# Token-routed experts whose fill and end are reordered, with the last router products reversed, and a chunked recurrence solved on four quadrants of the array

## The chip, the cores and the metric

One core of one Trainium2 chip runs the whole program in one launch. The metric is the device time of one execution in microseconds (us): the median of three runs. TensorE is called PE, VectorE DVE, ScalarE ACT, GpSimd POOL, and SyncE, which issues most transfers, SP.

## The reference

The reference is two model blocks in a row on a sequence of 1024 tokens of width 1024. Of the first block, two places matter here. `x @ w_out` gives a residual; its norm goes through a router (36 columns: 4 groups and 32 experts), and every token goes to 2 of 32 experts of hidden width 512:

```python
y = (silu(x @ w_gate[e]) * (x @ w_up[e])) @ w_down[e]      # for each token, its 2 experts
```

Of the second block, what matters is an RWKV recurrence over 8 heads of 64 x 64 in two directions:

```python
def rwkv_step(S, inp):
    r, w, k, v, kk, a = inp
    sa = einsum('dbhvk,dbhk->dbhv', S, -kk)
    S = S * w[..., None, :] + sa[..., :, None] * (kk * a)[..., None, :] + v[..., :, None] * k[..., None, :]
    return S, einsum('dbhvk,dbhk->dbhv', S, r)
```

The kernel computes the recurrence in 16 chunks of 64 steps. Within a chunk the dependence of the steps on each other is a strictly triangular matrix N, and what is needed is its inverse (I - N)^-1, a product of (I + N^(2^i)) over six levels.

## The kernel before, in words

Stages follow each other; each one has its own buffers and a block in which the five engines run their own instruction lists and wait for each other by semaphores. Between two stages all engines meet.

**The stage "go"** (`deep_norm`, from L3906) is the product with `w_out`. Row tiles of 128 tokens go through it in pairs. For each row tile it also computes the norm, transposes it (`turn`, L4035), splits it into a high and a low part on ACT (L4125) and DVE (L4207), and takes the router's logits: 24 products, each with 128 x 128 values of the norm as the loaded weights and 36 router columns streamed. For the last pair all of this comes after the pair's products, with nothing beside it; DVE then copies the logits (L4243) and the stage is over.

**The stage "moe"** (`moe`, from L1436) runs one step per tile of 128 token rows, 33 steps here, in a loop; step j does the gate and up products of tile j and the down product of tile j-1. Step 0 is written out, the later ones are a loop with a test at each step (`steps`, L1479), on every engine. A product takes three PE passes (high x low, low x high, high x high, `products3`, L157 to L159), so all weights are split: ACT writes the high part (`high`, L1629) and DVE the low part (`half`, L1775), in two halves (q) of 128 x 2048 values for each of the three weights. The rest of a step on ACT: `Silu` of the gate product (L1644), the high parts of the turned activation (L1647) and of the turned token rows (L1650), half of the output y (L1655), and the issue of the store of y (L1662), which waits for both halves of y. On DVE: the low part of the activation (L1790), the product with the up half (L1794), the low part of the rows (L1796), the other half of y (L1801). SP issues the loads: the row tile (L1529), then the weights (L1520), each as its split buffer comes free. Before the tiles can be read, POOL scatters all token rows to their slots with 16 indirect transfers (L1813), which all count on one semaphore, `moved`. The rows being scattered lie where the high and low parts of the down weights are written later, so ACT waits for `moved` before its first split of down weights at the end of step 0, and DVE's follows from it; SP waits for `moved` at the end of step 0 too, before any load of step 1.

The order at the end of a step on ACT is: its half of y, the high part of the down weights (two instructions), the wait for both halves of y, the store. On DVE it is: the low part of the up weights, its half of y, the low part of the down weights.

**The stage "rs"** (`rw_scan`, from L2714) is the recurrence. Of each chunk there are 16 matrices (4 head pairs, 2 members, 2 directions). For a chunk PE does: `prepare` (L2815 to L2832), `score` (L2845), `output` (L2903), `solve` (L2913), level 0 of the next chunk's inverse (L2876, L2882), `update` (L2922, L2927), `values` (L2855), levels 1 to 5 (L2878 to L2882), and `ask` of the next chunk (L2890). A level has two groups (g); in each, a product Q of 64 x 64 values by a 128-column operand (the next power and the next partial inverse at once), and a product P of 64 columns (the power's transpose). Both members b of a matrix pair have input rows and output rows in the same half of the partitions, so the level products use two of the array's four 64 x 64 quadrants. ACT copies Q (L2973) and group 1's P (L2974), DVE group 0's P (L3020), and DVE adds the partial inverse (L3026). A level starts when the copies of the one before have landed. `prepare`, `ask` (L2890) and the products of L2832 take their input rows from one half and write to either, four quadrants in turn. Every product here is f32 and shows as two MATMUL records.

```python
                    for e in range(RP):
                        for b in range(2):
                            d, p, o, k = e // 2, e % 2 * 2 + b, home[b], g * RP + e
                            ...
                                pe.matmul(p_q[g][o, e], pm[o, k], qx[o, k], start=True, stop=True)
```

Of the kernel before, what the change touches and what calls it, by code (L numbers as in the profile page):

```python
# [21 lines left out]
ALU = mybir.AluOpType  # L22
# [1413 lines left out]
def moe(nc, logits, consts, tri_strict, ones, h2, h2_rows, xs, ys, gate2, slots, tile_exp, ident, w_gate, w_up, w_down):  # L1436
# [5 lines left out]
    with Stage(nc, "moe") as s:  # L1442
# [29 lines left out]
        moved = s.sem("moved", soft=True)  # L1472
# [33 lines left out]
        def _(sp):  # L1506
# [15 lines left out]

            def ahead(j, b, k, n_used):
# [3 lines left out]
                if not first:  # L1527
                    sp.wait_ge(turned, past(j))
                    sp.dma_start(x[:, 1 - b], xs.rearrange("(j p) n -> j p n", p=P)[j + 1],  # L1529
                                 cond=(n_used > j + 1)).then_inc(x_in[1 - b], 16)  # L1530
# [26 lines left out]
            steps(sp, 1, step)  # L1557
# [63 lines left out]
        def _(act):  # L1621
# [50 lines left out]
        def _(v):  # L1672
# [113 lines left out]
            def step(j, b, k, n_used):  # L1786
                first = isinstance(j, int) and j == 0
                if not first:
                    v.wait_ge(at_hi, past(j))
# [12 lines left out]
                low(d_hi, d_lo, wd, wd_hi, wd_lo, j + 1)  # L1802
# [3 lines left out]
        def _(pool):  # L1806
# [4 lines left out]
            for t in range(NT):  # L1811
                for k in range(2):
                    pool.indirect_dma_start(xs[:, :], bass.IndirectOffsetOnAxis(ap=slots[:, k, t:t + 1], axis=0),  # L1813
                                            h2_rows[:, t], None).then_inc(moved, 16)
# [899 lines left out]
def rw_scan(nc, vecs, vs3, first, first_in, vT, el, sc_mask, p_mask, ident, yT):  # L2714
# [11 lines left out]
    with Stage(nc, "rs") as s:  # L2726
# [4 lines left out]
        sc, pm, qx = s.sb("sc", [P, 2, ND, 2, P]), s.sb("pm", [P, ND, RC]), s.sb("qx", [P, ND, P])  # L2731
# [4 lines left out]
        (turned, v_turned, p0_done, scored, level, z_done, u_done, s_done, y_done, bk_ok, v_ok, u_ok, lv_q,  # L2736
         lv_p0, lv_p1, p0_ok, sc_ok, x1_ok, lv_dve, zs_ok, s_ok, y_ok) = (s.sem(n) for n in (
             "turned", "v_turned", "p0_done", "scored", "level", "z_done", "u_done", "s_done", "y_done", "bk_ok",
             "v_ok", "u_ok", "lv_q", "lv_p0", "lv_p1", "p0_ok", "sc_ok", "x1_ok", "lv_dve", "zs_ok", "s_ok", "y_ok"))
# [6 lines left out]
        p_q, p_p = [wide(n) for n in range(2)], [banks[:, 2 + n] for n in range(2)]  # L2746
# [26 lines left out]
        def q_level(n, lv, g):  # L2773
            return (n * (NL - 2) + lv) * 2 + g + 1

        def p_level(n, lv):
            return n * (NL - 1) + lv + 1

        def dve_level(n, lv, g):
            return (n * (NL - 1) + lv - 1) * 2 + g + 1  # L2780
# [21 lines left out]
        def _(pe):  # L2802
            def prepare(n):
# [6 lines left out]
                if n:  # L2810
                    for g in range(2):
                        pe.wait_ge(lv_dve, past(dve_level(n - 1, NL - 1, g)))
# [6 lines left out]
                if n:  # L2819
                    pe.wait_ge(lv_p0, past(p_level(n - 1, NL - 2)))  # L2820
# [5 lines left out]
                if n:  # L2826
                    pe.wait_ge(lv_p1, past(p_level(n - 1, NL - 2)))
# [31 lines left out]
            def raise_power(n, lv):  # L2859
                for g in range(2):  # L2860
                    if lv == 0:
                        pe.wait_ge(sc_ok, past(2 * n + 2))
                    else:
                        if lv < NL - 1:
                            pe.wait_ge(lv_q, past(q_level(n, lv - 1, g)))
# [1640 lines left out]
```

## Time and profile before

| | us |
|---|---|
| median of three runs (4133.52 to 4139.69) | 4139.14 |
| the profiled execution, its own time | 4142.12 |
| its span | 4140.3 |
| PE busy in the span | 3631.0 (88%) |
| DVE busy | 2830.5 (68%) |
| ACT busy | 1609.6 (39%) |
| mean granted clock of PE | 0.936 |

A row of the timeline gives the start and the duration in us, the engine, the line, the operation, the tiles written and read, and in brackets how long the engine was idle before it and what released it. A row with x2 or more merges neighbours: its duration runs from the first start to the last end. MATMUL durations hold some 0.22 us of pipeline, so products that start 0.03 us apart overlap. PEld is the load of weights. PEclk is the clock that PE was granted, as a share of 2.4 GHz.

### The profile page before, as it was taken

Reading aid. Unit: us, or ns where it says so; the run is one execution under the profiler, and the core shown is the slowest. Engines: PE = TensorE matmul, PEld = TensorE weight load, DVE = VectorE, ACT = ScalarE, POOL = GpSimd, SP = SyncE. Lnnn points to the kernel's source line nnn. Section 1 sums busy time; section 2 is a strip of 40 time slices with the busy share of each in tenths; the row PEclk is TensorE's granted clock in tenths of the full one; section 3 lists DMA queues with packets and bytes.
Section 4 is the critical chain, followed back from the end, with each engine's and each line's share of the span. In section 5 each row is a group of like instructions: output and inputs, shape, how many; then the busy total and the mean of one; then the engine's idle time right before and its main releaser. Section 6 shows DMA issues by size and latency. Waiting matters only on the chain. (4 is left out here: it accounts for less than half of the span.)

```text
span 4140.3 us, 62371 instructions
## 1 busy us (share of the span) xinstructions
PE 3631.0 (88%) x24735; PEld 2927.8 (71%) x24735; DVE 2830.5 (68%) x3464; ACT 1609.6 (39%) x2136; POOL 72.4 (2%) x56
## 2 busy tenths in 40 slices
PE   6999996879959999948999776649999897999897
PEld 4888885767848888836888432319997676888786
DVE  4775325977559999978886588685555557667356
ACT  3222212545537777754333120253333133322244
POOL 0000000000020000010000000000000000000000
PEclk8999998999969999978999888779999998999999
DMA  5942225536579999953332331340111332222565
GB/s 199 337 166 92 88 76 194 192 112 214 181 278 420 413 411 411 399 194 102 102 122 102 124 123 69 117 166 26 42 34 63 102 117 77 82 91 73 187 192 170
DMA packets 262498, 689.49 MB, mean 167 GB/s; under 512 B 30136, under 2 KB 126072, under 8 KB 235754
## 3 DMA queue, kind: packets, MB, share of 16 engines
q1 hardware_dynamic: 226474, 559.75, 37.8%
q10 hardware_dynamic: 20528, 67.11, 4.3%
q0 software_dynamic: 15248, 59.14, 3.9%
q8 instruction: 177, 2.90, 0.3%
q14 instruction: 71, 0.58, 0.0%
HBM read 530.81 MB, written 172.96 MB: 170 GB/s over the span
## 5 line engine op out<-in xcount | busy, mean ns | idle before, releaser
L157 PE MATMUL g_ps<-h1T_hi,g_w_lo 128*128 128x512 f32 x448 | 175.4, 392 | 6.9 <-DVE g_w_lo L356 6.9
L1775 DVE TENSOR_TENSOR moe_wg_lo<-moe_wg,moe_wg_hi 128x2048 fp32r<-128x2048 f32 x68 | 153.1, 2288 | 35.6 <-ACT moe_wg_hi L1629 35.5
L159 PE MATMUL g_ps<-h1T_hi,g_w_hi 128*128 128x512 f32 x448 | 174.8, 390 | 0.0
L158 PE MATMUL g_ps<-h1T_lo,g_w_hi 128*128 128x512 f32 x448 | 174.8, 390 | 0.0
L4164 DVE TENSOR_TENSOR x3T_lo<-fd_w_raw,x3T_hi 128x1024 fp32r<-128x1024 f32 x66 | 80.8, 1224 | 122.6 <-ACT x3T_hi L4093 122.4
L1775 DVE TENSOR_TENSOR moe_wu_lo<-moe_wu,moe_wu_hi 128x2048 fp32r<-128x2048 f32 x68 | 152.9, 2288 | 16.3 <-ACT moe_wu_hi L1629 16.3
L1775 DVE TENSOR_TENSOR moe_wd_lo<-moe_wd,moe_wd_hi 128x2048 fp32r<-128x2048 f32 x66 | 148.3, 2289 | 14.9 <-ACT moe_wd_hi L1629 14.9
L2882 PE MATMUL rs_banks<-rs_pm,rs_qx 64*64 64x64 f32 x2048 | 157.2, 217 | 0.0
L157 PE MATMUL fd_acc<-x3T_hi,x3T_lo 128*128 128x512 f32 x352 | 139.2, 395 | 19.9 <-DVE x3T_lo L4167 19.9
L157 PE MATMUL g_ps<-x2T_hi,g_w_lo 128*128 128x512 f32 x352 | 139.8, 397 | 17.1 <-DVE g_w_lo L583 17.1
L157 PE MATMUL g_ps<-g_w_hi,h1T_lo 128*128 128x512 f32 x384 | 149.6, 390 | 0.0
L158 PE MATMUL g_ps<-g_w_lo,h1T_hi 128*128 128x512 f32 x384 | 149.4, 389 | 0.0
L159 PE MATMUL g_ps<-g_w_hi,h1T_hi 128*128 128x512 f32 x384 | 149.4, 389 | 0.0
L2882 PEld LDWEIGHTS rs_banks<-rs_pm,rs_qx 64*64 64x64 f32 x2048 | 143.6, 133 | 0.0
L158 PE MATMUL g_ps<-x2T_lo,g_w_hi 128*128 128x512 f32 x352 | 139.8, 397 | 0.0
L159 PE MATMUL g_ps<-x2T_hi,g_w_hi 128*128 128x512 f32 x352 | 139.2, 396 | 0.0
L158 PE MATMUL fd_acc<-x3T_lo,x3T_hi 128*128 128x512 f32 x352 | 138.7, 394 | 0.0
L159 PE MATMUL fd_acc<-x3T_hi 128*128 128x512 f32 x352 | 138.7, 394 | 0.0
L402 DVE COPY g_st<-g_ps 128x512 f32<-128x512 f32 x24 | 16.6, 691 | 176.4 <-PE g_ps L159 176.4
L1629 ACT ACTIVATE moe_wg_hi<-moe_wg 128x2048 fp32r<-128x2048 f32 x68 | 127.0, 1920 | 16.6 <-DMA moe_wg<-in_exp_w_gate 16.6
L4093 ACT ACTIVATE x3T_hi<-fd_w_raw 128x1024 fp32r<-128x1024 f32 x66 | 70.0, 1060 | 160.6 <-PE fd_acc L159 112.8
L2878 PE MATMUL rs_banks<-rs_qx,rs_pm 64*64 64x128 f32 x1536 | 131.2, 272 | 0.0
(738 smaller groups left out, 10776.4 us busy)
## 6 DMA issues: line engine op xcount, KB each, us to landing
moe_wg<-in_exp_w_gate SPq DMA_DIRECT2D x68, 1024.0 KB
moe_wu<-in_exp_w_up SPq DMA_DIRECT2D x68, 1024.0 KB
moe_wd<-in_exp_w_down SPq DMA_DIRECT2D x66, 1024.0 KB
fd_w_raw<-in_ffn_w_down SPq DMA_DIRECT2D x66, 512.0 KB, 4.5
go_w_raw<-in_w_out SPq DMA_DIRECT2D x64, 512.0 KB, 4.4
g_w<-in_w_in SPq DMA_DIRECT2D x52, 512.0 KB, 4.8
g_w<-in_w_in SPq DMA_DIRECT2D x22, 1024.0 KB, 7.7
s_xs<-g_zero POOLq DMA_DIRECT2D x2, 8192.0 KB, 34.3
```

The lines of the kernel that those rows point to most:

```text
L157: pe.matmul(out, l[1], r[0], start=(k == 0), stop=False)
L158: pe.matmul(out, l[0], r[1], start=False, stop=False)
L159: return pe.matmul(out, l[0], r[0], start=False, stop=(k == kt - 1))
L402: v.tensor_copy(st[:, j % 2, 2 * i + 1], ps[:, 2 * i + 1]).then_inc(by_dve, 1)
L1629: act.activation(hi[:, q * m:q * m + m], w[:, q * m:q * m + m], ACT.Copy).then_inc(sem_hi, 1)
L1775: v.tensor_tensor(lo[:, q * m:q * m + m], w[:, q * m:q * m + m], hi[:, q * m:q * m + m], ALU.subtract).then_inc(sem_lo, 1)
L2878: pe.matmul(p_q[g][o, e], pm[o, k], qx[o, k], start=True, stop=True)
L2882: mm = pe.matmul(p_p[g][o, e], q, pm[o, k], start=True, stop=True)
L4093: act.activation(w_hi[:, n % NB], w_raw[:, n % NR], ACT.Copy).then_inc(w_high, 1)
L4164: v.tensor_tensor(w_lo[:, n % NB], w_raw[:, n % NR], w_hi[:, n % NB], ALU.subtract).then_inc(w_low, 1)
```

## The change

In "moe": `moved` becomes two semaphores, one for the first eight scatter transfers and one for the last eight. ACT's and DVE's splits of the down weights go from the end of step j to the start of step j+1, behind a wait for `moved[0]` on ACT and `moved[1]` on DVE. At the end of a step ACT waits that the down weights have landed and for y, and issues the store. SP's step 1 is written out; in it the load of row tile 2 stands behind four weight loads and behind the wait for both `moved`. In "go": the products of the last pair load the router's 36 columns as weights and stream 128 rows; ACT copies the result and PE transposes it into the logits. In "rs": for one of two head groups (`par` 1) the halves of the partitions alternate with the level, so that the products of a level go to four quadrants; all products have 64 columns, in three kinds (P, its transpose Q, and the partial inverse X = X(I + N^(2^i)), for which DVE makes `rx` = power + I); the copies are one of 128 x 384 for each group and parity, three on ACT and one on DVE. The groups g are now the directions.

```diff
@@ moe @@
-        moved = s.sem("moved", soft=True)
+        moved = [s.sem(f"moved{n}", soft=True) for n in range(2)]
@@ sync: ahead() and step() @@
-                if not first:
+                if not isinstance(j, int):
                     sp.wait_ge(turned, past(j))
-                    sp.dma_start(x[:, 1 - b], ...).then_inc(x_in[1 - b], 16)
+                    rows_x(j, b, n_used)
...
+                if isinstance(j, int) and j == 1:
+                    sp.wait_ge(turned, past(j))
+                    for m in moved:
+                        sp.wait_ge(m, 16 * NT)
+                    rows_x(j, b, n_used)
                 for q in range(2):
                     if not first:
                         sp.wait_ge(d_lo, past(j * 2 + (q - 1)))
...
-                if isinstance(j, int) and j == 0:
-                    sp.wait_ge(moved, 16 * 2 * NT)
...
-            steps(sp, 1, step)
+            steps(sp, 2, step)
@@ scalar: step() @@
+                if not first:
+                    act.wait_ge(moved[0], 16 * NT)
+                    high(d_in, d_hi, wd, wd_hi, j * 16)
                 act.wait_ge(gated, past(j + 1))
...
                     act.activation(y[:, 1 - b, 0:512], p_y[:, 0:512], ACT.Copy).then_inc(y_act, 1)
+                for q in range(2):
+                    act.wait_ge(d_in[q], past(j * 16 + 16))
                 if first:
-                    act.wait_ge(moved, 16 * 2 * NT)
-                high(d_in, d_hi, wd, wd_hi, j * 16 + 16)
+                    act.nop()
                 if not first:
                     act.wait_ge(y_act, past(j + 1))
                     act.wait_ge(y_dve, past(j + 1))
@@ vector: step() @@
                 if not first:
+                    v.wait_ge(moved[1], 16 * NT)
+                    low(d_hi, d_lo, wd, wd_hi, wd_lo, j)
                     v.wait_ge(at_hi, past(j))
...
                     v.tensor_copy(y[:, 1 - b, 512:], p_y[:, 512:]).then_inc(y_dve, 1)
-                low(d_hi, d_lo, wd, wd_hi, wd_lo, j + 1)
@@ rw_scan @@
-        p_q, p_p = [wide(n) for n in range(2)], [banks[:, 2 + n] for n in range(2)]
+        def powers_of(g, par):
+            return banks[:, 2 * g + par]...[:, 0:6 * RC]...
+        def place(b, par, lv):
+            return other[b] if par and lv % 2 else home[b]
@@ tensor: raise_power() @@
+                    else:
+                        pe.wait_ge(lv_act, past(act_at(n, lv - 1, 3 if g else 1)))
+                        if g == 0:
+                            pe.wait_ge(lv_dve, past(dve_at(n, lv - 1)))
+                    members = [(par * RP + g * 2 + a, a, b, par) for a in range(2) for par in range(2) for b in range(2)]
...
+                    if lv < NL - 1:
+                        for k, a, b, par in members:
+                            mm = pe.matmul(to(a, b, par, 0), power(k, a, b, par), pm[place(b, par, lv), k], start=True, stop=True)
+                    if lv < NL - 2:
+                        for k, a, b, par in members:
+                            mm = pe.matmul(to(a, b, par, 1), pm[place(b, par, lv), k], power(k, a, b, par), start=True, stop=True)
+                    if lv:
...
+                        pe.wait_ge(lv_r, past(r_at(n, lv - 1, g)))
+                        for k, a, b, par in members:
+                            o = place(b, par, lv)
+                            mm = pe.matmul(to(a, b, par, 2), rx[o, k], xm[o, k], start=True, stop=True)
@@ scalar: raise_power() @@
+                for g, par in ((0, 0), (1, 0), (1, 1)):
                     act.wait_ge(level, past(at_level(n, lv, g)))
+                    act.activation(own(px[:, :, c], g, par), powers_of(g, par)[:, :, c], ACT.Copy).then_inc(lv_act, 1)
@@ vector: raise_power() @@
+                v.tensor_copy(own(px[:, :, c], 0, 1), powers_of(0, 1)[:, :, c]).then_inc(lv_dve, 1)
+                if lv < NL - 1:
+                    v.drain()
+                    for g in range(2):
+                        v.wait_ge(lv_act, past(act_at(n, lv, 3 if g else 1)))
+                        ...
+                        v.tensor_tensor(both[0], both[1], bc(eye...), ALU.add).then_inc(lv_r, 1)
@@ deep_norm: tensor, last pair @@
-                for t in passes[-1]:
-                    rate(t)
+                for i, t in enumerate(passes[-1]):
+                    pe.wait_ge(by_dve, past(t + 1))
+                    for k in range(ND):
+                        mm = products3(pe, acc[0:nf, t % n_acc, 0:P], [h[:, k] for h in (f_hi, f_lo)],
+                                       [h[:, t % 2, k] for h in (t_hi, t_lo)], k, ND)
+                    mm.then_inc(pair_done, 1)
+                for i, t in enumerate(passes[-1]):
+                    pe.wait_ge(pair_ok, past(i + 1))
+                    mm = pe.transpose(pl[:, t, 0:nf], pair[0:nf, t % 2], ident[0:nf, 0:nf])
+                mm.then_inc(rated, 1)
```

## Rows read from the trace of the kernel before

**Rows 1.** Windows: us, then busy us (count) of PE, PEld, DVE, ACT, POOL; PEclk, DMA, GB/s
```profile
1145.00:1158.00 13.00, 12.00 (x56) 11.92 (x56) 1.72 (x3) 1.02 (x1) 0.00 (x0) 0.50 0.01 1
...
1245.00:1797.00 552.00, 552.00 (x2591) 458.84 (x2589) 505.19 (x309) 415.53 (x307) 0.00 (x0) 1.00 0.95 389
...
2790.00:3175.00 385.00, 373.39 (x10242) 357.86 (x10239) 217.06 (x449) 125.37 (x304) 0.00 (x0) 0.99 0.10 31
```

**Rows 2.** Timeline of one step of the experts on ACT and DVE
```profile
1780.03 3.71 ACT L1629 ACTIVATE moe_wd_hi<-moe_wd 128x2048 fp32r<-128x2048 f32 x2
1781.12 0.68 DVE L1801 COPY moe_y<-moe_p_y 128x512 f32<-128x512 f32 x1
1781.97 4.49 DVE L1775 TENSOR_TENSOR moe_wd_lo<-moe_wd,moe_wd_hi 128x2048 fp32r<-128x2048 f32 x2 [0.17 <-ACT moe_wd_hi L1629]
1782.02 0.34 ACTq L1662 DMA_DIRECT2D s_ys<-moe_y  x1
...
1787.90 4.50 DVE L1775 TENSOR_TENSOR moe_wg_lo<-moe_wg,moe_wg_hi 128x2048 fp32r<-128x2048 f32 x2 [0.83 <-ACT moe_wg_hi L1629]
...
1794.62 4.49 DVE L1775 TENSOR_TENSOR moe_wu_lo<-moe_wu,moe_wu_hi 128x2048 fp32r<-128x2048 f32 x2 [0.49 <-ACT moe_wu_hi L1629]
```

**Rows 3.** Line L1801, DVE's half of y: all instructions, ns min/median/max, first and last start
```profile
L1801 DVE COPY moe_y<-moe_p_y x32: 680/684/685, 1243.3 to 1799.0; 128x512 f32<-128x512 f32 x32
```

**Rows 4.** Timeline at the experts' fill, ACT
```profile
1220.51 3.71 ACT L1629 ACTIVATE moe_wd_hi<-moe_wd 128x2048 fp32r<-128x2048 f32 x2 [9.99 <-DMA s_xs<-h_rows,slots]
```

**Rows 5.** Timeline at the experts' end: the next stage's first instruction
```profile
1809.17 0.35 SPq L1874 DMA_DIRECT2D nf_r<-s_x  x1
```

**Rows 6.** Timeline of the last router products
```profile
1146.71 0.38 PE L157 MATMUL go_pl<-go_f_hi,go_t_lo 128*128 128x36 f32 x1
...
1148.16 1.22 DVE L4207 TENSOR_TENSOR go_t_lo<-go_pt,go_t_hi 128x1024 fp32r<-128x1024 f32 x1 [3.18 <-ACT go_t_hi L4125]
...
1157.16 0.46 DVE L4243 COPY logits<-go_pl 128x288 f32<-128x288 f32 x1 [7.78 <-PE go_pl L159]
```

**Rows 7.** Timeline of one chunk of the recurrence: where its levels lie
```profile
2937.79 0.33 PE L2876 MATMUL rs_banks<-rs_sc,rs_pm 64*64 64x64 f32 x4
...
2938.00 1.21 ACT L2980 ACTIVATE rs_uv<-rs_p_z 64x512 f32<-64x512 f32 x2 [3.50 <-PE rs_p_z L2913]
...
2939.80 1.15 PE L2922 MATMUL rs_p_s<-rs_uv,rs_bk 128*64 128x64 f32 x32
...
2942.57 0.33 PE L2878 MATMUL rs_banks<-rs_qx,rs_pm 64*64 64x128 f32 x2
...
2943.96 0.43 PE L2878 MATMUL rs_banks<-rs_qx,rs_pm 64*64 64x128 f32 x4
...
2944.21 0.38 ACT L2973 ACTIVATE rs_qx<-rs_banks 128x256 f32<-128x256 f32 x1 [3.65 <-PE rs_banks L2882]
...
2951.40 0.42 DVE L3026 TENSOR_TENSOR rs_qx<-rs_qx,rs_banks 128x256 f32<-128x256 f32 x1 [0.92 <-ACT rs_qx L2973]
...
2951.97 0.34 PE L2880 MATMUL rs_banks<-rs_qx,rs_pm 64*64 64x64 f32 x4 [0.16 <-DVE rs_qx L3026]
...
2955.02 0.37 PE L2815 MATMUL rs_banks<-k_ident,rs_cm 64*128 64x64 f32 x5
```

**Rows 8.** Timeline: 64 x 64 products on four quadrants (L2832) and on two (L2903, L2913)
```profile
2956.97 0.34 PE L2832 MATMUL rs_banks<-rs_cm 64*64 64x64 f32 x9
...
2959.84 0.50 PE L2903 MATMUL rs_banks<-rs_cm,rs_st 64*64 64x64 f32 x10
...
2960.36 1.10 PE L2913 MATMUL rs_p_z<-rs_zs,rs_qx 64*64 64x64 f32 x32
```

**Rows 9.** Lines of ACT and DVE in one chunk: busy us, mean ns | idle before
```profile
L2973 ACT ACTIVATE rs_qx<-rs_banks 128x256 f32<-128x256 f32 x8 | 3.1, 382 | 8.3 <-PE rs_banks L2882 8.3
...
L2959 ACT ACTIVATE rs_bk<-rs_banks 128x512 f32<-128x512 f32 x2 | 1.1, 595 | 2.2 <-PE rs_banks L2815 2.2
...
L3020 DVE COPY rs_pm<-rs_banks 128x256 f32<-128x256 f32 x5 | 2.1, 422 | 1.9 <-PE rs_banks L2882 1.9
```

More of the change, by code:

```diff
@@ L2730, in rw_scan @@
         bk, uv = s.sb("bk", [P, 2, ND, P]), s.sb("uv", [P, 2, ND, 2, RC])
-        sc, pm, qx = s.sb("sc", [P, 2, ND, 2, P]), s.sb("pm", [P, ND, RC]), s.sb("qx", [P, ND, P])
+        sc, px = s.sb("sc", [P, 2, ND, 2, P]), s.sb("px", [P, ND, 3 * RC])
+        pm, qm, xm = (px[:, :, c * RC:c * RC + RC] for c in range(3))
+        rx, eye = s.sb("rx", [P, ND, RC]), s.sb("eye", [P, RC])
         zs, st = s.sb("zs", [P, ND, RC]), s.sb("st", [P, ND, RC])
@@ L2771, in at_level, with act_at, dve_at, r_at @@
             return (n * NL + lv) * 2 + g + 1
[L2773 to L2780, printed above, removed]
+        def act_at(n, lv, i):
+            return (n * NL + lv) * 3 + i
+        def dve_at(n, lv):
+            return n * NL + lv + 1
+        def r_at(n, lv, g):
+            return (n * (NL - 1) + lv) * 2 + g + 1
+        def columns(lv):
+            return slice(0, 2 * RC) if lv == 0 else slice(0, 3 * RC) if lv < NL - 1 else slice(2 * RC, 3 * RC)
+        def own(ap, g, par):
+            return ap[:, par * RP + 2 * g:par * RP + 2 * g + 2]
         home = [half[1], half[0]]
         other = [half[0], half[1]]
+        def place(b, par, lv):
+            return other[b] if par and lv % 2 else home[b]
         units = [(2 * a + b, a, b, q ^ b) for a in range(RP // 2) for q in range(2) for b in range(2)]
@@ L2810, in prepare @@
                 if n:
-                    for g in range(2):
-                        pe.wait_ge(lv_dve, past(dve_level(n - 1, NL - 1, g)))
+                    pe.wait_ge(lv_act, past(act_at(n - 1, NL - 1, 3)))
+                    pe.wait_ge(lv_dve, past(dve_at(n - 1, NL - 1)))
                 for d in range(2):
@@ L2907, in solve @@
                 pe.wait_ge(zs_ok, past(j + 1))
-                for g in range(2):
-                    pe.wait_ge(lv_dve, past(dve_level(j, NL - 1, g)))
+                pe.wait_ge(lv_act, past(act_at(j, NL - 1, 3)))
+                pe.wait_ge(lv_dve, past(dve_at(j, NL - 1)))
                 for d in range(2):
@@ L2968, in raise_power @@
             def raise_power(n, lv):
-                for g in range(2):
-                    k = slice(g * RP, g * RP + RP)
+                c = columns(lv)
+                for g, par in ((0, 0), (1, 0), (1, 1)):
                     act.wait_ge(level, past(at_level(n, lv, g)))
-                    if lv < NL - 2:
-                        act.activation(qx[:, k, 0:RC], p_q[g][:, :, 0:RC], ACT.Copy).then_inc(lv_q, 1)
-                act.activation(pm[:, k], p_p[1][:, 0:RP], ACT.Copy).then_inc(lv_p1, 1)
+                    act.activation(own(px[:, :, c], g, par), powers_of(g, par)[:, :, c], ACT.Copy).then_inc(lv_act, 1)
             def solved(j):
@@ L2982, in _ @@
             prepare(0)
-            for lv in range(NL - 1):
+            for lv in range(NL):
                 raise_power(0, lv)
@@ L2989, in _ @@
                 if j + 1 < NRC:
-                    for lv in range(NL - 1):
+                    for lv in range(NL):
                         raise_power(j + 1, lv)
@@ L2995, in _ @@
             v.memset(st[:, :, :], 0.0).then_inc(s_ok, 1)
+            for o in half:
+                v.tensor_copy(eye[o], ident[o, o])
+            v.drain()
             v.wait_ge(m_in, past(32))
@@ L2999, in prepare @@
                 v.wait_ge(p0_done, past(n + 1))
-                v.tensor_tensor(by_parity(pm[:, :, :]), banks[:, 3:5, 0:RP], by_parity(mp[:, :, :]), ALU.mult).then_inc(p0_ok, 1)
+                v.tensor_tensor(by_parity(pm), banks[:, 3:5, 0:RP], by_parity(mp[:, :, :]), ALU.mult).then_inc(p0_ok, 1)
                 if n >= 2:
@@ L4156, in _ @@
                     high(t)
+                for i, t in enumerate(g):
+                    act.wait_ge(pair_done, past(i + 1))
+                    act.activation(pair[0:nf, t % 2], acc[0:nf, t % n_acc, 0:P], ACT.Copy).then_inc(pair_ok, 1)
         @block.vector
```

73 lines of the change are left out of this document (30 added, 43 removed).

## The prediction

> **What bounds the kernel now.** I read the windows by stage first, because the change touches three stages with different limits. In the experts' steady part [rows 1] PE is busy for 552.00 of 552.00 us at the full clock, with DVE at 505.19 (92%) and DMA at 0.95. So PE bounds it, but DVE has only 8% to spare. In the recurrence [rows 1] PE is busy for 373.39 of 385.00 us, and DVE and ACT are far below. In the window of the last router products PE is busy too, but at 0.50 of the clock. Next the timelines. In one step of the experts [rows 2] the reader is to see how tightly ACT's high part of the down weights (1780.03) sits before DVE's low part (1781.97): DVE idles 0.17 us there, 0.83 before the gate weights and 0.49 before the up weights, 1.49 us a step in all. DVE's half of y repeats 32 times from 1243.3 to 1799.0 [rows 3]: 31 periods of 17.92 us.
>
> **The change, part by part.**
>
> *Experts, every step.* Before, ACT starts the high part of the down weights right after its own half of y and only then waits for DVE's half. After, the wait for DVE's half and the store stand ahead of it. DVE's half ends at 1781.12 + 0.68 = 1781.80; the store's issue ends at 1782.02 + 0.34 = 1782.36 [rows 2], so 0.56 us. Then the loop's test. No row shows a boundary with work behind it: from the DVE's last split (1799.0 + 0.68 + 4.49 = 1804.2, [rows 2, 3]) to the next stage at 1809.17 [rows 5] lie 15 empty passes, 0.33 us each at least; above, ACT's trace leaves room for 1.0. I take 0.6, as registers are computed too. Then the first high half, 1.91 (1780.03 to just before 1781.97, [rows 2]), and 0.03 of signal. DVE, which has nothing else to do at that point, idles 3.1 us in place of 0.17. Its other two gaps vanish, since ACT gets ahead of a later DVE: ACT would finish the gate half some 7.7 us after DVE's y, DVE asks for it at 8.2. DVE's own work from the start of the down split (1781.97) to the end of y (1799.0 + 0.68 = 1799.7) is 17.74 - 0.83 - 0.49 = 16.42. The period becomes 16.42 + 3.1 = 19.5 us, longer than PE's 17.92: DVE is the bound and PE waits for the split rows. That is 1.6 us a step and +50 us over 31 periods (ends: +40 with 0.3 for the test, +62 with 1.0). The added wait for the landed down weights costs nothing: their buffer is free once DVE's split has read it, 5 to 8 us into the period, and the wait stands at its end. Were they late, the store, the next high half and DVE behind it would be.
>
> *Experts, the fill.* ACT's 9.99 us of idle for the scatter [rows 4] goes, but DVE still waits for the last scatter at the start of step 1, with the low parts of the down and gate weights, the rows and y queued behind it, and SP's load of row tile 2 waits too. From that landing (1220.5) the DVE chain is the 16.42 from above, so y of step 1 would end at 1236.9 against 1243.3 + 0.68 = 1244.0: -7. Against it: SP now issues four weight loads of 1 MB (tile 2's) before the scatter has landed; at 389 GB/s [rows 1] they are worth 10.8 us of the same DMA engines, which could put the landing back by as much, +4. On POOL nothing is moved. I take -1, nearer to the late end, since the scatter's last transfers are issued while these loads run.
>
> *Experts, the end.* DVE's and ACT's splits of weights for a tile that doesn't exist go. DVE ends 4.49 us earlier, but ACT has 15 passes of its own after the store: 0 to -4.5, taken as -2.
>
> *Last router products.* 48 products run from 1146.71 to shortly before 1157.16 [rows 6], 0.213 us each at half clock, the pace of their 128-column weights. Reversed, 128 columns stream: a 512-column product takes 552/2591 = 0.213 at the full clock [rows 1], so 0.107 for 128 at half. The second tile can't start before its low part, 1148.16 + 1.22 = 1149.38 [rows 6]; 24 x 0.107 brings 1151.9, and the copy, a transpose and the pipeline some 1.6: 1153.5, -3.6. If the small weights load as slowly as the large, it is +1. I take -3; what follows on DVE is serial, so it reaches the end.
>
> *Recurrence, the rate.* Records on four quadrants start (0.34 - 0.22)/8 = 0.015 us apart (L2832), on two 0.031 (L2903) and 0.028 (L2913) [rows 8]; two records a product: 0.031 against 0.058. The products of a mid level are 48 of 64 columns now, where they were 16 of 128 and 16 of 64: 1.5 us of PE, where a level takes 2 x 1.35 = 2.7 us now (a group is 2943.96 back to about 2942.6, [rows 7]).
> A rule speaks against this. After the change two row halves write the same bank at the same time. L2903 does this already, at 0.031 against 0.028 for L2913, which alternates banks [rows 8]: it costs a tenth, not the gain. The Trainium skill (TensorEngine Tiling (Array Packing), Gotcha 1: PSUM Pressure) says that different row tiles cannot access the same PSUM bank simultaneously; by that the levels would stay at 0.058, a rival below.
>
> *Recurrence, the chain.* At this rate PE waits for copies. From the end of a group to ACT's start is 0.25 (2943.96 to 2944.21); from a DVE end (2951.82) to PE 0.15 [rows 7]. ACT copies 256 columns in 0.38, 512 in 0.60, so 384 in 0.49; DVE 0.42 and 0.68, so 0.56 [rows 3, 9]. Group 1 needs two ACT copies in a row, 0.88 with their overlap. Its cycle in levels 2 and 3: 0.25 + 0.88 + 0.15 + 24 x 0.031 = 2.0, plus 0.1 for DVE's sum with I, which X waits for: 2.1. In levels 4 and 5 that sum is bare: 0.25 + 0.88 + 0.03 + 0.42 + 0.15 + 0.25 = 2.0 each. Levels 1 to 5: 1.5 + 2.1 + 2.1 + 2.0 + 2.0 = 9.7, and `prepare` follows 0.9 later, after the last copies: 10.6 against 2955.02 - 2942.57 = 12.45 [rows 7]. -1.85 x 16 = -30. Level 0 runs from 2937.79 to 2939.80; `update` then needs ACT's copies, 2938.00 + 1.21 + 0.15 = 2939.36: -0.44 x 15 = -6. DVE's four small sums instead of two lie beside level 0. Sum -36. Ends: +18 if the products keep 0.058 (level slots 2.8, the chain behind levels 4 and 5), -90 if no copy were ever waited for.
>
> **The sum.** +50 - 1 - 2 - 3 - 36 = +8 us. The profiled execution took 4142.12, which gives 4150; it lies 3 us over the median of the runs, 4139.14, so the median comes to 4147.
>
> **The rivals.**
> *The experts' period stays PE's* (faster). It needs DVE's wait for the down split to stay under 1.49 us, its whole slack [rows 2]; against it stands the 1.91 of the high half alone. Sum -42: 4097. Chance 0.10.
> *The recurrence's chain is shorter than its copies read*: if a copy of 384 columns costs what one of 256 does and starts earlier, a level comes to 1.8, another -19, at the far end PE's own 1.5. It decides from 3.3 us saved a chunk. 4128, 4093 at the end of it. Chance 0.13.
> *Four quadrants don't pay* (slower): same-bank writes, or PE's clock granted at half in the new gaps, where it is 0.99 now. +18 for -36: 4201. Chance 0.10.
> *The forecast*: the loop stretches, the recurrence pays back most of it. 0.67, spread 4130 to 4168.
>
> **How the numbers follow.** A measurement of this kernel can tell 0.2% from no change, 8.3 us. The forecast lies on that edge: of its 0.67, 0.32 is slower, 0.31 the same, 0.04 faster. With the rivals: faster 0.04 + 0.10 + 0.10 = 0.24, same 0.31 + 0.03 = 0.34, slower 0.32 + 0.10 = 0.42. The range 4108 to 4170 leaves out the first rival and the last, 2 in 10.
>
> **What would show it.** In the experts: DVE's half of y every 19.5 us, the wait of DVE's down split for ACT's near 3 us a step, PE no longer busy throughout, the steady part near 600 us. In the recurrence: level records 0.015 to 0.02 apart, a chunk in 21.2 us where it took 23.5, ACT's copies as the releaser of level products. The logits' copy 3 us sooner after L4207. If y still comes every 17.9 us, the forecast is wrong and the kernel is faster by about 1%.

## The result and the profile after

The changed kernel takes 4187.14 us (median of 3, 4185.75 to 4189.05) against 4139.14 before: a ratio of 1.0114, interval 1.0098 to 1.0129. It is slower by 48 us, where 8 were forecast, and outside the range of 4108 to 4170. Its profiled span is 4185.4 us, 45.1 over that of before.

I read the windows by stage first. The columns are those of [rows 1].

```profile
1136.00:1148.00 12.00, 7.54 (x66) 6.79 (x66) 5.45 (x7) 2.65 (x5) 0.00 (x0) 0.72 0.27 107
1240.00:1832.00 592.00, 565.10 (x2577) 456.58 (x2575) 499.63 (x308) 414.02 (x310) 0.00 (x0) 1.00 0.94 359
2822.00:3222.00 400.00, 321.98 (x11760) 291.96 (x11760) 230.98 (x496) 164.66 (x384) 0.00 (x0) 0.92 0.10 30
```

The reader is to see two things. In the experts' steady part, 592 us where 552 were enough [rows 1], PE is no longer busy throughout. In the recurrence PE was busy for 373.39 of 385.00 us at a granted clock of 0.99; now it is busy for 321.98 of 400.00 at 0.92, for 15% more instructions, and the stage is longer. Since 1.00 and 0.50 are the clock's two levels, 0.92 means that about 16% of the stage, 64 us, ran at half.

The timeline of the experts, DVE in two steps:

```profile
1796.27 0.68 DVE L1814 COPY moe_y<-moe_p_y 128x512 f32<-128x512 f32 x1
1800.13 4.50 DVE L1786 TENSOR_TENSOR moe_wd_lo<-moe_wd,moe_wd_hi 128x2048 fp32r<-128x2048 f32 x2 [3.18 <-ACT moe_wd_hi L1636]
...
1815.68 0.68 DVE L1814 COPY moe_y<-moe_p_y 128x512 f32<-128x512 f32 x1
1819.30 4.50 DVE L1786 TENSOR_TENSOR moe_wd_lo<-moe_wd,moe_wd_hi 128x2048 fp32r<-128x2048 f32 x2 [2.94 <-ACT moe_wd_hi L1636]
```

And ACT in the same two:

```profile
1797.19 0.34 ACTq L1673 DMA_DIRECT2D s_ys<-moe_y  x1
1798.18 3.72 ACT L1636 ACTIVATE moe_wd_hi<-moe_wd 128x2048 fp32r<-128x2048 f32 x2 [5.74 <-issue]
...
1816.60 0.34 ACTq L1673 DMA_DIRECT2D s_ys<-moe_y  x1
1817.36 3.72 ACT L1636 ACTIVATE moe_wd_hi<-moe_wd 128x2048 fp32r<-128x2048 f32 x2 [5.50 <-DVE moe_y L1814]
```

DVE's copy of y ends at 1796.95, the store is issued at 1797.19, ACT's split of the down weights starts at 1798.18 and DVE's at 1800.13. DVE waits 3.18 or 2.94 us there, and nowhere else in the step: from 1800.13 to the end of the next copy, 1816.36, it works for 16.23 us. The line of the copy, its first and last start:

```profile
L1814 DVE COPY moe_y<-moe_p_y x32: 680/684/687, 1236.8 to 1834.9; 128x512 f32<-128x512 f32 x32
```

31 periods from 1236.8 to 1834.9 are 19.29 us each, against 17.92 [rows 3]. From the timeline, the logits' copy, the fill's first row on DVE and the next stage's first instruction, which answer to [rows 4 to 6]:

```profile
1147.71 0.46 DVE L4289 COPY logits<-go_pl 128x288 f32<-128x288 f32 x1 [2.32 <-PE go_pl L4117]
...
1221.22 4.49 DVE L1786 TENSOR_TENSOR moe_wd_lo<-moe_wd,moe_wd_hi 128x2048 fp32r<-128x2048 f32 x2 [18.35 <-DMA s_xs<-h_rows,slots]
...
1842.84 0.34 SPq L1886 DMA_DIRECT2D nf_r<-s_x  x1
```

The timeline of a stretch of levels in the recurrence, rows of PE and one of ACT's copies:

```profile
2979.72 0.46 PE L2903 MATMUL rs_banks<-rs_px 64*64 64x64 f32 x16
2980.00 0.29 PE L2906 MATMUL rs_banks<-rs_px 64*64 64x64 f32 x6
2983.15 0.39 PE L2906 MATMUL rs_banks<-rs_px 64*64 64x64 f32 x10 [2.86 <-issue]
2983.32 0.45 PE L2913 MATMUL rs_banks<-rs_px,rs_rx 64*64 64x64 f32 x16
2983.55 0.45 PE L2903 MATMUL rs_banks<-rs_px 64*64 64x64 f32 x16
...
2983.81 1.25 ACT L3003 ACTIVATE rs_px<-rs_banks 128x384 f32<-128x384 f32 x3 [3.54 <-PE rs_banks L2913]
...
2984.73 0.54 PE L2903 MATMUL rs_banks<-rs_px 64*64 64x64 f32 x16 [0.26 <-ACT rs_px L3003]
2985.03 0.67 PE L2906 MATMUL rs_banks<-rs_px 64*64 64x64 f32 x16
2985.46 0.67 PE L2913 MATMUL rs_banks<-rs_px,rs_rx 64*64 64x64 f32 x16
2985.88 0.43 PE L2903 MATMUL rs_banks<-rs_px 64*64 64x64 f32 x5
2987.16 0.58 PE L2903 MATMUL rs_banks<-rs_px 64*64 64x64 f32 x10 [0.85 <-issue]
```

Outside the pauses the rate is the forecast's: 16 records of L2903 and L2913 start (0.45 - 0.22)/15 = 0.015 us apart, 0.031 a product, and by the starts of the sets at 2983.32 and 2983.55 it is 0.029. But in the middle of a set of products whose operands are all there, PE stops for 2.86 us and waits for "issue", that is, for nothing that the profile shows. ACT waits 3.54 us behind it. Behind the pause the rate is the one of the half clock for a while: the set at 2983.32 is followed by the next 0.23 us later, the one at 2985.03 only 0.43 later. The window from there on, in the columns of [rows 1], has the granted clock at half:

```profile
2985.00:2995.20 10.20, 8.54 (x211) 7.50 (x204) 3.76 (x9) 4.10 (x11) 0.00 (x0) 0.50 0.02 4
```

The waits of the stage, us in total, times, longest:

```profile
ACT rs_px L3003 <- PE rs_banks L2913: 146.4, 123, 4.4
DVE rs_rx L3059 <- ACT rs_px L3003: 63.3, 64, 4.2
PEld rs_banks L2913 <- issue: 20.1, 21, 3.4
PEld rs_banks L2913 <- ACT rs_px L3003: 17.2, 22, 1.4
```

The copies wait for PE far more than PE waits for them. I then counted PE's instructions along the trace: weight loads, matmuls and the few of its sequencer. A pause here is the time from one instruction's start to the next one's. The pauses for nothing stand whole multiples of 256 instructions apart; four of them:

```
number of the instruction   start, us   pause, us
31802                        2983.15     3.08
32058                        2987.16     1.16
33338                        3009.14     1.41
33594                        3012.63     0.64
```

The DMA queues of the stage give the other half of it, queue and kind: packets, MB, share. First before, then after:

```profile
q8 instruction: 81, 1.33, 1.4%
```

```profile
q8 instruction: 93, 1.52, 1.6%
```

A packet is 1.52 MB / 93 = 16 KB, and 93 x 256 is 23808, where PE's records of the stage are 23776; before it is 81 x 256 = 20736 to 20718. So PE's program comes in blocks of 256 instructions over a DMA queue of its own, one packet each, and no two of them start less than 3.3 us apart in either trace. A product of 64 x 64 shows as two weight loads and two matmuls. Four quadrants want 256 instructions, 64 products, in 64 x 0.031 = 2.0 us. In the records of the stage PE stands still for over 0.5 us 78 times, 83.6 us in all; before 3 times, 4.0 us. Of the 78, 31 with 47.2 us are put down to "issue", and every one of them stands at the same place in the count of 256. Most of the others are waits for a copy.

### The profile page after: what moved, and what is told of

Same layout as the page of the kernel before. It is cut to its first block and busy times, and to the rows that moved or that the text cites. A ratio compares the mean times of both kernels' runs of the same rounds, so it can differ in the third digit from the quotient of the medians.

```text
span 4185.4 us, 65587 instructions
## 1 busy us (share of the span) xinstructions
PE 3578.4 (85%) x26273; PEld 2849.5 (68%) x26273; DVE 2835.4 (68%) x3512; ACT 1640.8 (39%) x2216; POOL 71.8 (2%) x56
## 5 line engine op out<-in xcount | busy, mean ns | idle before, releaser
L1786 DVE TENSOR_TENSOR moe_wd_lo<-moe_wd,moe_wd_hi 128x2048 fp32r<-128x2048 f32 x64 | 143.8, 2289 | 113.3 <-ACT moe_wd_hi L1636 94.9
L1636 ACT ACTIVATE moe_wd_hi<-moe_wd 128x2048 fp32r<-128x2048 f32 x64 | 119.1, 1908 | 179.8 <-issue 89.1
L3003 ACT ACTIVATE rs_px<-rs_banks 128x384 f32<-128x384 f32 (+2 forms) x288 | 111.4, 434 | 152.9 <-PE rs_banks L2913 146.4
L4210 DVE TENSOR_TENSOR x3T_lo<-fd_w_raw,x3T_hi 128x1024 fp32r<-128x1024 f32 x66 | 80.8, 1224 | 120.8 <-ACT x3T_hi L4136 120.6
L157 PE MATMUL fd_acc<-x3T_hi,x3T_lo 128*128 128x512 f32 x352 | 139.2, 395 | 18.1 <-DVE x3T_lo L4213 18.1
L1636 ACT ACTIVATE moe_wu_hi<-moe_wu 128x2048 fp32r<-128x2048 f32 x68 | 126.6, 1918 | 0.7 <-DMA moe_wu<-in_exp_w_up 0.7
```

The lines of the kernel that those rows point to most:

```text
L157: pe.matmul(out, l[1], r[0], start=(k == 0), stop=False)
L1636: act.activation(hi[:, q * m:q * m + m], w[:, q * m:q * m + m], ACT.Copy).then_inc(sem_hi, 1)
L1786: v.tensor_tensor(lo[:, q * m:q * m + m], w[:, q * m:q * m + m], hi[:, q * m:q * m + m], ALU.subtract).then_inc(sem_lo, 1)
L3003: act.activation(own(px[:, :, c], g, par), powers_of(g, par)[:, :, c], ACT.Copy).then_inc(lv_act, 1)
L4210: v.tensor_tensor(w_lo[:, n % NB], w_raw[:, n % NR], w_hi[:, n % NB], ALU.subtract).then_inc(w_low, 1)
```

## The experiments

The theories: the experts lose by the order of store and split; the recurrence's gain is lost to **supply**, blocks of instructions that come too slowly. The rivals: **contention** of four quadrants for the PSUM banks, a chain of waits that the new scan makes longer, or an effect of the three parts on each other.

**The parts alone.** Each is the kernel before with that part of the diff.

```diff
+ mm = products3(pe, acc[0:nf, t % n_acc, 0:P], ...)            # router alone: deep_norm's hunks
...
+ act.wait_ge(moved[0], 16 * NT); high(d_in, d_hi, wd, wd_hi, j * 16)    # experts alone: its hunks
...
+ return other[b] if par and lv % 2 else home[b]                # scan alone: rw_scan's hunks
```

> The kernel before with the reversed last router products alone. In the changed kernel the logits' copy came 9.5 us sooner, 4.0 of it already there at the first of these products and 5.5 gained in them. If the 5.5 are the reversal's (products at 0.107 us, then 0.060 once the clock is full), this run is 5 to 6 us faster than before, about 4134, and the whole stage after it moves with it. If instead the 4 us ahead of it belong to the change too, it is 9 us faster. Rival: the work of the experts' start waits for weights, not for the logits, and the run is within 2 us of before.

> The kernel before with the experts' reordering alone. My theory: the store's wait ahead of ACT's high part stretches the period of a step from 17.92 to 19.29 us, as in the changed kernel, 31 periods, +42 us; the fill costs +3 (the scatter lands 10 us later, the waits gone give 7 back), the end gives -2. Sum +43: 4182. Rival, DMA: the period is long because weights arrive late; then ACT's and DVE's waits for DMA would show tens of us in the steady part, and the sum could lie anywhere. Rival, cross effect of the other parts: this run alone would be well under +43.

> The kernel before with the recurrence on four quadrants alone. Instruction supply theory: PE's instructions come in blocks of 256, one per 3.3 us at best; the dense level products use one up in 2 to 2.6 us, so PE stands still at every 256th instruction. The stage then takes 17 us more, as in the changed kernel, with stalls of 1 to 3.5 us at multiples of 256 PE records: total +14 to +20, 4155. Chain theory (the copies' chain is longer than I read): the same loss, but spread over every level as waits for ACT or DVE, none at multiples of 256. Rival: in the changed kernel the loss came from the other two parts (shifted phases); then this run is at 36 us under before.

Measured, as medians beside before's 4139.33: router 4133.82 (ratio 0.9986, 0.9976 to 0.9995); experts 4182.31 (1.0108, 1.0091 to 1.0125); scan 4152.56 (1.0024, 1.0002 to 1.0046). The differences, -5.5, +43.0 and +13.2, add to +50.7, where the whole change has +48.0. The 2.7 between the sums is less than the intervals leave open, so no effect of the parts on each other shows. Two of the three lose, the scan by an interval that only just leaves out no change: one of its five runs was at 4134.97. Weights that come late are out as a cause of the experts' loss: in the steady steps of the experts alone DVE waits 31 times, 94.9 us in all, for ACT's down split, and no wait for a DMA is listed.

**Bursts.** Ahead of the recurrence's first chunk 512 products run whose operands have been there for long, on four quadrants, then 512 on two. Nothing waits for a copy.

```diff
+            for rep in range(32):
+                ... pe.matmul(banks[home[b], 3 + par, d * 2 + a], vec(...), vec(...))    # four quadrants
+            for rep in range(32):
+                ... pe.matmul(banks[half[par], 2, d * RP + p], vec(...), vec(...))       # two
```

> The kernel before with two bursts of PE work ahead of the recurrence, whose results are overwritten: 512 products of 64 x 64 by 64 on four quadrants, then 512 on two quadrants. Each product is 4 PE instructions (2 loads of weights, 2 passes), so each burst is 2048 instructions, 8 blocks of 256. Supply theory: the first burst begins at the short-run pace of 0.031 us a product, then falls to the pace of the blocks, 3.3 to 3.6 us per 64 products (0.052 to 0.056 each), with pauses at every 64th product, 26 to 29 us in all; the second, at 0.058 a product or 3.7 us per block, hardly pauses, 30 us. Rival, no supply limit: the first burst keeps 0.031 to 0.036 throughout, 16 to 18 us, and the second 30.

Measured: 4196.62 us in one run; the bursts took 28.0 and 30.6 us. In the first, with the idle before them:

```profile
2794.68 0.27 PE L2936 MATMUL rs_banks<-rw_first 64*64 64x64 f32 x2 [0.51 <-issue]
...
2798.16 0.27 PE L2936 MATMUL rs_banks<-rw_first 64*64 64x64 f32 x2 [1.38 <-issue]
...
2801.90 0.27 PE L2936 MATMUL rs_banks<-rw_first 64*64 64x64 f32 x2 [1.65 <-issue]
...
2805.65 0.27 PE L2936 MATMUL rs_banks<-rw_first 64*64 64x64 f32 x2 [1.65 <-issue]
```

```
instructions of the burst at which PE pauses:  429  685  941  1197  1453  1709  1965   (256 apart)
pause, us:                                    0.73 1.59 1.87  1.87  1.60  1.59  1.59
a product, us:  four quadrants 0.034 between the pauses, 0.055 with them
                two quadrants  0.059 between the pauses, 0.060 with them (0.6 us in all)
```

In the first burst the granted clock was 0.50 for the first 4.7 us; from the second pause on a product takes 0.029 us between the pauses ((3.74 - 1.87)/64). Contention gives no reason for pauses every 256 instructions; supply does. The rate that four quadrants hold is 0.055 us a product, 28.0 / 8 = 3.5 us a block of 64. That is hardly better than the 0.060 of two. (The expectations below call a pair of one weight load and one matmul a product; a product of mine is two such pairs, so their 27.3, 16.8 and 29.3 ns are my 0.055, 0.034 and 0.059 us.)

**A loop around the bursts.** Each burst as 4 passes over 128 products, two blocks.

```diff
-            for rep in range(32):
+            with pe.Fori(0, 4):
+                for rep in range(8):
```

> The kernel with the two bursts of 1024 products each ahead of the recurrence, but each burst a loop of 4 passes over 256 products (512 instructions, two blocks of 256). Written out, the burst on four quadrants took 28.0 us, 27.3 ns a product, with a pause of 1.6 to 1.9 us every 256 instructions and 16.8 ns a product between them. Theory: the pauses are the fetch of a block of instructions. In a loop of two blocks the first pass pays them and the later ones do not: 7 + 768 x 0.0168 = 20 us for the first burst (up to 24 with the loop's own jumps), with no fetches in it after the first pass; the second burst, on two quadrants, stays at 29 to 30 ns a product. Rival: the pauses are the array's or the queue's own, every 256 instructions whatever their source: 28 us as before.

Measured: the first burst took 18.4 us in place of 28.0. Its first pass still went at 0.054 us a product with one pause of 0.96, and with the granted clock at 0.50 for its first 4.3 us; the passes behind it at 0.029, with 0.15 us at each jump. The windows of both bursts, first written out, then looped:

```profile
2788.60:2816.80 28.20, 18.80 (x1027) 17.82 (x1029) 0.00 (x0) 0.00 (x0) 0.00 (x0) 0.91 0.15 52
2816.80:2847.30 30.50, 30.34 (x1031) 30.04 (x1023) 0.00 (x0) 0.00 (x0) 0.00 (x0) 1.00 0.02 5
```

```profile
2794.30:2812.90 18.60, 17.72 (x1025) 17.46 (x1025) 0.00 (x0) 0.00 (x0) 0.00 (x0) 0.88 0.22 75
2812.90:2843.00 30.10, 30.10 (x1034) 30.03 (x1028) 0.00 (x0) 0.00 (x0) 0.00 (x0) 1.00 0.00 1
```

The instruction queue over the two bursts, in the same order:

```profile
q8 instruction: 16, 0.26, 1.8%
```

```profile
q8 instruction: 4, 0.07, 0.5%
```

The same products, the same banks, a quarter of the packets, and past the first pass the pauses are gone. So they are not a stop every 256 instructions whatever their source. Two quadrants gain nothing from the loop. The total, 4197.42, does not show it: the looped kernel came to the burst 5.7 us later, left the recurrence 4.6 us earlier, and the rest went in later stages that the edit does not touch.

**The scan on two quadrants.** The new scan's instructions in the same order, every operand in its home half.

```diff
-            return other[b] if par and lv % 2 else home[b]
+            return home[b]
```

> Before with the new scan, but every level's operands stay in their home half: the same instructions in the same order, on two quadrants in place of four. Theory: instructions come to TensorE at no more than 256 in 3.4 us, 27 ns for a product of two instructions, and on two quadrants a product takes 29 ns: four quadrants gain next to nothing, so this kernel is at most 6 us slower than the one on four, 4150 to 4159 us. Rival: the four quadrants do gain what the burst shows between its pauses (16.8 against 29.3 ns a product), and the loss is elsewhere: 16 chunks of some 200 products by 12 ns, 38 us slower than on four, over 4180 us.

Measured: 4158.31 us (1.0048, 1.0034 to 1.0062), 5.7 behind the scan on four. As written, four quadrants are worth 5.7 us by the medians, which the spread of the runs hardly separates (4135 to 4156 against 4155 to 4161), and 10.4 by the stage in the profiled runs (393.5 against 403.9); the forecast had them worth 54 (-36 against +18). On two quadrants only 5 pauses over 0.5 us are left that go to "issue", 5.6 us in place of 41.6.

**The scan in a loop.** TensorE's levels 1 to 4 as two passes over two levels, so that two levels' instructions a chunk need no fetching. Level 4 then computes one product more than it needs, and the waits whose value depends on the pass stand on instructions of their own. The flat kernel is its control, the same but for the loop.

```diff
+            def raise_powers(n):
+                with pe.Fori(0, 2) as i:          # flat: for i in range(2)
+                    for lv in (1, 2):
+                        raise_power(n, lv, i)     # waits for values of level lv + 2 * i
+                raise_power(n, NL - 1)
...
-                    for lv in range(1, NL):
-                        raise_power(j + 1, lv)
+                    raise_powers(j + 1)
```

> Before with the new scan, TensorE's levels 1 to 4 written as a loop of two passes over two levels (level 4 then computes one product more than it needs); the four waits of a group stand on instructions of their own. It takes about 190 instructions a chunk out of what is fetched (of some 1490), 13.4 ns each, 2.6 us of a chunk. Theory: the pauses every 256 instructions are what took the scan's gain, so the stage gets shorter than the written-out scan's by 10 to 35 us of its 399: 4117 to 4145 us in all (written out 4152.6), and fewer pauses over 0.5 us in TensorE's records. Rival: the pauses lie beside waits for the copies and cost the chain nothing: 4152 or, with the loop's jumps and the added waiting instructions (16 chunks by about 0.5 us), up to 4162.

> The same kernel as the one with the loop, with its two passes written out: the same products, the same waiting instructions, nothing looped. Both theories: 4153 to 4165 us, the written-out scan's 4152.6 and some more instructions (32 of products and some 16 waits a chunk, at 13.4 ns, 16 chunks: 10 us). Its difference to the looped kernel is the loop's alone: by the fetch theory 15 to 40 us, by the rival none or below nothing.

Measured: looped 4137.63 us (0.9997, 0.9988 to 1.0007), flat 4183.34 (1.0103, 1.0084 to 1.0122). The loop alone is worth 45.7 us, more than I had expected, since the flat kernel lost 31 us to its added instructions and not 10. Against the scan as it was written it is 15 us. The instruction queue of the stage, looped and then flat:

```profile
q8 instruction: 74, 1.21, 1.3%
```

```profile
q8 instruction: 97, 1.59, 1.5%
```

The stage took 372.9 us looped and 428.3 flat; 393.5 for the scan as written, 382.2 before. The pauses over 0.5 us come to 57.6 us looped (there are real waits for copies among them), 94.3 flat, 80.8 as written. Those put down to "issue" alone are 22.9 us looped, 60.0 flat and 41.6 as written. This is the same kernel with 23 blocks fewer to fetch, so supply is shown to be what turned the scan's gain into a loss. It is not shown that the whole -36 would come without it: the looped stage is 9.3 us shorter than before's, and how the rest divides between the pauses that are left, the extra product, the half clock and the copies' chain stays open. The granted clock moves with the pauses: in 350 us from 2800 on, first looped, then flat:

```profile
2800.00:3150.00 350.00, 294.65 (x11681) 271.46 (x11685) 219.31 (x474) 156.24 (x364) 0.00 (x0) 0.98 0.09 30
```

```profile
2800.00:3150.00 350.00, 280.39 (x10335) 256.81 (x10325) 192.89 (x414) 137.82 (x322) 0.00 (x0) 0.90 0.10 31
```

Over the whole stage the clock was granted at half for 18.1 us looped, 100.5 flat, 55.4 as written, 4.8 before, and 3.9 on two quadrants, where the pauses are few as well. How much of the 45.7 is the pauses themselves and how much the half clock behind them, no run separates; if work at half clock takes twice as long, the 82 us less of it are worth at most 41 (an estimate).

**The loop on two quadrants.** The looped scan with `place` as in the scan on two.

> The looped scan on two quadrants: every operand stays in its home half, everything else as in the looped kernel. Written out, two quadrants stood 5.7 us behind four (4158.3 to 4152.6), 10.4 in the profiled stages (403.9 to 393.5). Theory: four quadrants gain more once fewer instructions have to be fetched, since on two the array (29 ns a product) and not the fetch sets the pace, so there the loop brings little: 4153 to 4165 us, 15 to 27 behind the looped kernel's 4137.6. Rival: the loop helps both alike (it is a gain of its own, not one that frees the quadrants): 4143 us, 6 behind.

Measured: 4177.41 us (1.0091, 1.0074 to 1.0108), 40 behind the loop on four. That is over my 15 to 27, because I had not priced level 4's extra product: L2894, as that line was numbered there, is 1536 matmuls and 62.0 us busy in the scan on two quadrants, and L2898 here 2048 and 85.8, so up to 24 us, as PE is busy for 329.44 of 350 us here; on four quadrants the same is 53.0 to 62.4. So the 40 hold by estimate some 14 us that are the product's and not the fetch's. The rest, 25, still stands against 5.7 in the written-out pair: four quadrants pay once the instructions are there. No written-out kernel with the extra product ran on two quadrants, so the split of the 40 is an estimate.

**The order of store and split.** Before, with the wait for y and the store ahead of ACT's split; the split stays at the end of the step.

```diff
-                high(d_in, d_hi, wd, wd_hi, j * 16 + 16)
                 if not first: ... (waits for both halves of y, store)
+                high(d_in, d_hi, wd, wd_hi, j * 16 + 16)
```

> Before, with one change: at the end of a step ACT waits for both halves of y and issues the store ahead of its split of the down weights, not behind it. Theory: this order alone is what the experts' steady steps lost. In the run with the experts' reordering alone DVE's half of y ends at 1517.7 us, the store's issue is at 1517.9, ACT's split starts at 1518.66 and DVE's at 1520.60, 2.93 us behind the copy's end, and DVE then works 16.2 us without a longer wait up to the end of the next copy: the period is 19.2. The same is to be seen here: 31 periods of 19.2 in place of 17.92, +38 to +42, about 4179 us. Rival: the place of the split at the head of the step (and the later transfer of the weights) costs the time, and the order of store and split little: under 4150.

Measured: 4170.59 us (1.0078, 1.0062 to 1.0093), +32, less than the 38 to 42 expected. The period is 18.86 us; 31 x 0.94 are 29, and the next stage starts 12.6 us behind the last copy of y in place of 10.1. The timeline shows what is left out:

```profile
1507.32 0.68 DVE L1801 COPY moe_y<-moe_p_y 128x512 f32<-128x512 f32 x1
1510.63 4.49 DVE L1775 TENSOR_TENSOR moe_wd_lo<-moe_wd,moe_wd_hi 128x2048 fp32r<-128x2048 f32 x2 [2.62 <-ACT moe_wd_hi L1629]
...
1508.22 0.34 ACTq L1661 DMA_DIRECT2D s_ys<-moe_y  x1
1508.68 3.72 ACT L1629 ACTIVATE moe_wd_hi<-moe_wd 128x2048 fp32r<-128x2048 f32 x2 [5.17 <-DVE moe_y L1801]
```

From the store's issue to the split's start it is 0.46 here and 0.76 or 0.99 in the changed kernel, where the loop's test and registers lie between them. So of the 1.37 us a step, 0.94 is the order of store and split, and 0.43, by what is left over, the split's place at the head of the next step.

**After with the old steady steps.** The new fill, then each step as before.

```diff
-                if not first:                       # high(d) / low(d) at the head of every step
+                if isinstance(j, int) and j == 1:   # of step 1 alone
...
+                    high(d_in, d_hi, wd, wd_hi, j * 16 + 16)     # at the end of the others, low(d) too
```

> After, with the steps from 1 on as before (ACT's and DVE's split of the down weights at the end of the step, ahead of the store's issue); the fill as after, step 1 written out. Theory: the period goes back to 17.92 and the 42 us come back, less about 2 that the old end costs: 4145 to 4152 us, 4149 taken (before 4139, router -5.5, scan +13, fill +3). Rival: the loss hangs on the fill's new state (the split of tile 0 at the head of step 1, two semaphores): the period stays over 19 and the time over 4175.

Measured: 4147.25 us (1.0021, 1.0012 to 1.0031). The period is back at 17.85 and 40 us have come back. The loss was in the steady steps, not in the fill.

**Router and loop together.**

> The looped scan and the reversed router products together. They lie in stages apart, so their differences add: the looped scan's time less 5.5 us. If the loop brings back 20 us, 4127 us, below both kernels; if nothing, 4147.

Measured: 4129.96 us (0.9978, 0.9969 to 0.9988), where the looped scan less the router's 5.5 gives 4132; it is 8.8 below before and 57 below the changed kernel: the best of all that ran, if by little.

## Why the prediction was wrong

By steps, against the profile after:

| step | predicted | measured | from |
|---|---|---|---|
| experts, 31 periods | +50 | +42.4 | 31 x (19.29 - 17.92) |
| fill | -1 | +3.0 | y of step 1, with the logits' copies aligned: 89.1 us behind them, 86.1 before |
| end | -2 | -2.2 | next stage 8.0 behind the last y copy, 10.1 before |
| router | -3 | -5.5 | first product to logits' copy 4.98, 10.45 before |
| recurrence | -36 | +17.3 | stage 399.5, 382.2 before |

They add to +55; the spans differ by 45.1, and the other 10 are in three stretches without any edit, all shorter (4.0 ahead of the router products, 2.3 between the experts and the recurrence, 3 behind it). Stretches without an edit move by as much in other runs, 5.7 in the looped burst, so I read nothing into them. The same holds within the table: the fill's 86.1 is 84.8 to 88.5 in the runs that leave it as it was and 88.4 to 89.4 in the three with the new one, so its cost is nearer 2. And the same new scan took 393.5 us in the kernel with the scan alone and 401.2 in the one with the old steady steps, so the recurrence's +17.3 can be anything from +11 to +19.

**The step that failed is the recurrence's chain**, at its first words: "At this rate PE waits for copies." The rate of 0.031 us a product came from nine records of L2832 [rows 8], a set short enough to lie inside one block. It was right, and it is there in the profile after; it does not last. I priced what a product costs the array and never what it costs the program: 48 products a level are 192 instructions, and the whole stage went from 20718 to 23776. The evidence was in the trace of before, in the instruction queue's packets. The chunk came to 24.8 us (mean of 15 periods) in place of 21.2, and +17 lies at the end +18 that I gave to products that keep 0.058 us, for another reason than the one I had in mind.

**The rival "four quadrants don't pay"** came nearest, with 4201 and a chance of 0.10. Its size was right and neither of its mechanisms was the first cause: two row halves do write one bank in the new levels, as they did in the old ones, and between pauses they go at 0.029 to 0.031 us a product, where the looped burst, with a bank for each row half, had 0.029. The Trainium skill's rule on it (TensorEngine Tiling (Array Packing), Gotcha 1: PSUM Pressure) would have kept two quadrants' 0.058; the trace does not agree with it. The half clock did come, 65 us of it and 0.92 over the stage; the one in the timeline above lies behind a pause, and with few pauses there was next to none.

**The rival of a shorter chain** did not come true: no chunk period was under 22.9 us. With the pauses in the way, the length of the copies' chain itself was not tested.

**The experts' step** was right in mechanism and 8 us too large. Predicted were 16.42 us of DVE's work and 3.1 of waiting; measured are 16.23 and 2.94 or 3.18. The 16.42 probably held short waits for signals, which vanish when ACT runs ahead; 31 x 0.2 is 6 us. The wait, the loop's test at 0.6 (0.65 in the slower of two steps) and the vanished second and third gaps were as forecast. The rival of an unchanged period is out.

**The fill** fell near its late end. The scatter lands at 1221.2 against 1220.5, though the logits came 9.5 us earlier; with the experts' reordering alone, the logits unmoved, DVE's wait for it ends at 1231.2, 10.7 later, and I had priced the four loads of tile 2's weights at 10.8. That it is these loads was argued and fits in size, but no run took them away.

**The router** gained more, since the clock rose to full at about 1145.2, with the first tile's last products: the second tile's start 0.060 us apart in place of 0.107. The end was right.

## What to carry to other kernels

A dense run of small instructions has two prices, the array's and the program's: divide the time by the instructions, and where it comes to less than some 14 ns each over more than a block of 256, the fetch sets the pace. A faster placement then gains little (5.7 us here in place of 54), an edit that adds instructions loses, and a loop over two levels, whose body was not fetched again, is what paid here. On a step whose slack is 1.5 us, no wait for the other engine's last result may stand ahead of the work that this engine needs next: issue the store behind it.

## What I had not expected of the hardware

TensorE's instructions came in blocks of 256, one DMA packet of 16 KB each, and never less than 3.2 us apart, 3.5 in the dense burst, 13.7 ns an instruction. Past a loop's first pass a product on four quadrants took 0.029 us, with 0.15 at a jump. The Trainium skill (Runtime: NRT & Kernel Launch, Instruction fetch mechanics) gives the block of 256 too, but calls the cost of crossing one mostly hidden and says that kernels prefer full unrolling where possible. Here a crossing cost 1.6 to 1.9 us in the dense burst, and the unrolled scan was 45.7 us slower than the looped one.
